# Two transformer blocks in float32 on one core: the out-projection of the first block's mixers taken over from float32 matmuls by three rounded passes

## What is computed

```python
h = rms_norm(x, mix_norm_g[l])
proj = jnp.einsum("bsd,dc->bsc", h, w_in[l])
moba_p, mla_p, sb_p, ssm_p = _split(proj, (MOBA_COLS, MLA_COLS, SB_COLS, SSM_COLS))
o_moba = moba_mixer(...); o_mla = mla_mixer(...)
o_sb = stick_breaking_mixer(sb_p); o_ssm = mamba2_mixer(...)
heads = rms_norm(jnp.stack([o_moba, o_mla, o_sb], axis=2), head_out_g[l])
mixed = jnp.concatenate([heads.reshape(bsz, seq, 3 * GROUP_WIDTH), o_ssm], axis=-1)
x = x + jnp.einsum("bsc,cd->bsd", mixed, w_out[l])
...                                   # then the feed-forward part of the layer
```

## Time and profile before

| | |
|---|---|
| three runs, median (lowest to highest) | 1769.16 us (1768.7 to 1773.98) |
| the profiled execution, its own time | 1764.72 us |
| span in the trace, first to last instruction | 1762.9 us |
| mean granted TensorE clock | 0.999 |
| TensorE matmul busy | 1747.6 us, 99% of the span |
| VectorE busy | 1191.3 us, 68% |
| ScalarE busy | 830.6 us, 47% |
| float32 matmuls of the out-projection (L892) | 256 records in two layers |

### The profile page before, as it was taken

The page is one execution under the profiler, slowest core; times in us unless marked ns, Lnnn a source line. Parts: engine busy times, 40 slices in busy tenths (PEclk is TensorE's granted clock), DMA queues, the critical chain, the costliest instruction groups (busy, mean ns, idle before and its releaser), DMA issues.

```text
span 1762.9 us, 32830 instructions
## 1 busy us (share of the span) xinstructions
PE 1747.6 (99%) x13378; PEld 1670.4 (95%) x13378; DVE 1191.3 (68%) x1863; ACT 830.6 (47%) x1108; POOL 29.2 (2%) x16
## 2 busy tenths in 40 slices
PE   8999999999999999999999999999999999999999
PEld 7879999988899999999989888999999999899999
DVE  6867886467698856766468623767556765777763
ACT  5656554356565544343345443343443344554442
POOL 0000000000000000000051000000000000000000
PEclk9999999999999999999999999999999999999999
DMA  6132556433145554455333422445444453335553
GB/s 257 73 144 106 195 183 224 168 112 143 72 168 190 209 205 167 169 190 186 127 134 144 168 84 96 169 183 208 166 156 178 167 203 144 109 138 194 188 211 122
DMA packets 36491, 284.28 MB, mean 161 GB/s; under 512 B 5040, under 2 KB 7344, under 8 KB 9008
## 3 DMA queue, kind: packets, MB, share of 16 engines
q1 hardware_dynamic: 36400, 283.00, 44.2%
HBM read 281.93 MB, written 1.05 MB: 161 GB/s over the span
## 4 chain that ended last, share of the span: by engine, by line
PE 88%; DVE 8%; ACT 2%; issue 1%; DMA 0%; SPq 0%; ACTq 0%; DVEq 0%
PE PS L1423 24%; PE PS L1428 24%; PE PS L1424 24%; PE PS L892 3%; PE PS L1301 3%; PE PS L727 1%; PE PS L771 1%; PE PS L748 1%; PE PS L1190 1%; PE PS L1089 0%; PE PS L916 0%; PE PS L1365 0%; DVE W L2577 0%; PE PS L1367 0%; PE PS L1371 0%
## 5 line engine op out<-in xcount | busy, mean ns | idle before, releaser
L1423 PE MATMUL PS<-Hhi,split 128*128 128x272 f32 (+1 forms) x2216 | 548.4, 286 | 0.0
L1424 PE MATMUL PS<-Hlo,split 128*128 128x272 f32 (+1 forms) x2120 | 520.1, 284 | 0.0
L2192 DVE TENSOR_TENSOR split<-wa,split 128x2048 fp32r<-128x2048 f32 (+2 forms) x174 | 358.7, 2061 | 123.9 <-ACT split L1567 123.9
L1423 PEld LDWEIGHTS PS<-Hhi,split 128*128 128x128 f32 x2216 | 416.4, 188 | 1.0 <-issue 0.4
L1424 PEld LDWEIGHTS PS<-Hlo,split 128*128 128x128 f32 x2120 | 399.1, 188 | 0.3
L1567 ACT CAST split<-wa 128x2048 fp32r<-128x2048 f32 (+2 forms) x174 | 299.3, 1720 | 63.9 <-PE PS L1428 61.4
L1428 PE MATMUL PS<-Hhi,split 128*128 128x256 f32 (+1 forms) x2080 | 274.8, 285 | 0.0
L1423 PE MATMUL PS<-hidhi,split 128*128 128x256 f32 (+1 forms) x1088 | 268.1, 285 | 0.5 <-DVE hidlo L2873 0.5
L1424 PE MATMUL PS<-hidlo,split 128*128 128x256 f32 (+1 forms) x1088 | 267.4, 284 | 0.0
L1428 PEld LDWEIGHTS PS<-Hhi,split 128*128 128x128 f32 x2080 | 261.9, 188 | 0.0
L1423 PEld LDWEIGHTS PS<-hidhi,split 128*128 128x128 f32 x1088 | 205.0, 188 | 1.0 <-DVE hidlo L2873 0.9
(11 more groups left out here) (422 smaller groups left out, 2380.5 us busy)
## 6 DMA issues: line engine op xcount, KB each, us to landing
wa<-in_wfi SPq DMA_DIRECT2D x126, 1024.0 KB, 4.8
wa<-in_wfo SPq DMA_DIRECT2D x48, 1408.0 KB, 6.1
wa<-in_wmix SPq DMA_DIRECT2D x25, 2048.0 KB, 7.9
wa<-in_wmix SPq DMA_DIRECT2D x4, 1536.0 KB, 6.4
H<-in_wfi SPq DMA_DIRECT2D x3, 1024.0 KB, 10.2
G<-in_wfi SPq DMA_DIRECT2D x3, 1024.0 KB, 5.0
wa<-in_wmix SPq DMA_DIRECT2D x2, 1024.0 KB, 4.7
wa<-in_wmix SPq DMA_DIRECT2D x1, 1824.0 KB, 7.6
```

What stands on the lines that cost most here:

```text
L1423: pe.matmul(o, hi, xhi, start=first, stop=False)
L1424: pe.matmul(o, hi, xlo, start=False, stop=False)
L2192: dve.tensor_tensor(out=wlo[n % 2][:, at:width], in0=wa[:, c % 2, at:width], in1=whi[n % 2][:, at:width].bitcast(F32), op=ALU.subtract).th ...
```

## The change

The out-projection goes over to rounded parts. Its weights become eight further pieces (numbers 16 to 23), one for each side and branch in the order of `OUT1`; ScalarE rounds each (`round_piece`) and VectorE forms its rest (`rest_piece`), placed by hand in the two streams. Two new places, M (over `Hlo`) and K (further on in `hidhi`), join A and B. Each branch's normed output is rounded by ScalarE (`round_branch`) and its rest formed by VectorE (`rest_of_branch`). On TensorE `rounded_rows` does hi*hi and lo*hi (16 matmuls) and `remaining_rows` hi*lo (8 matmuls), in place of the 8 float32 matmuls of `out_rows`. No DMA is added or removed, and the conditions on which slots are refilled stay (the out-projection's last matmuls of a side). First the tables and TensorE's stream:

```diff
+OUT1 = [(0, 2), (0, 1), (1, 2), (1, 1), (0, 3), (1, 3), (0, 0), (1, 0)]
+
 PIECES1 = [(1, 2), (1, 3), (2, 0), (2, 1), (2, 2), (2, 3), (3, 0), (3, 1), (3, 2), (3, 3), (4, 0), (4, 1), (4, 2), (4, 3), (5, 0), (5, 1)]
 
-PLACES1 = "AE" + "BCGH" + "AEBC" + "AEBG" + "EB"
+OUT_AT = len(PIECES1)
+PIECES1 = PIECES1 + [(6 + side, group) for side, group in OUT1]
+
+PLACES1 = "AE" + "BCGH" + "AEBC" + "AEBG" + "EB" + "AMBKAMBK"
+
+OUT_SPLITS = 1 + len(OUT1) // 2
...
+                def split_at(group):
+
+                    groups = [g for side, g in OUT1 if side == 0]
+                    return l * OUT_SPLITS + 2 + groups.index(group)
+
+                def rounded_rows(side, group, first=False):
+
+                    n = OUT_AT + OUT1.index((side, group))
+                    hi, lo = halves(n, 2)
+                    pe.wait_ge(S.mx_xhi, split_at(group))
+                    pe.wait_ge(S.mx_hi, pieces + n + 1)
                     for j in range(4):
-                        m = 4 * side + j
-                        for k in ks:
-                            mm = pe.matmul(out_place(m), wo[side][:, k, P * j:P * j + P], MIX[:, k, 0:SEQ],
-                                           start=first and m % 2 == 0 and k == ks[0], stop=last and k == ks[-1],
-                                           skip_group_check=True)
-                        if last and m % 2:
+                        for i in range(2):
+                            pe.matmul(out_place(4 * side + j), hi[:, i, P * j:P * j + P], Xhi[:, 2 * group + i, :],
+                                      start=first and j % 2 == 0 and i == 0, stop=False, skip_group_check=True)
+                    pe.wait_ge(S.mx_lo, pieces + n + 1)
+                    for j in range(4):
+                        for i in range(2):
+                            pe.matmul(out_place(4 * side + j), lo[:, i, P * j:P * j + P], Xhi[:, 2 * group + i, :],
+                                      start=False, stop=False, skip_group_check=True)
+
+                def remaining_rows(side, group, last=False):
+
+                    n = OUT_AT + OUT1.index((side, group))
+                    hi, _lo = halves(n, 2)
+                    pe.wait_ge(S.mx_xlo, split_at(group))
+                    for j in range(4):
+                        for i in range(2):
+                            mm = pe.matmul(out_place(4 * side + j), hi[:, i, P * j:P * j + P], Xlo[:, 2 * group + i, :],
+                                           start=False, stop=last and i == 1, skip_group_check=True)
+                        if last and j % 2:
                             mm.then_inc(S.prod_done, 1)
-
-                moba_rows, mla_rows, stick_rows, ssm_rows = ((2 * g, 2 * g + 1) for g in range(4))
+                    if not last:
+                        mm.then_inc(S.mx_used, 1)
...
                 soft_scores(moba, 0)
-                wo = [use(6, base, KD, P * PER1)]
-                pe.wait_ge(S.st_done, upto(S.st_done))
-                out_rows(0, stick_rows, first=True)
-                pe.wait_ge(S.ml_done, upto(S.ml_done))
+                take(2)
+                upto(S.st_done)
+                rounded_rows(0, 2, first=True)
+                upto(S.ml_done)
                 for h in range(4):
...
-                out_rows(0, mla_rows)
+                rounded_rows(0, 1)
+                remaining_rows(0, 2)
+                remaining_rows(0, 1)
                 soft_scores(moba, 1)
-                wo.append(use(7, base, KD, P * PER1))
                 pe.wait_ge(S.ssm_arg, upto(S.ssm_arg))
-                out_rows(1, stick_rows, first=True)
+                rounded_rows(1, 2, first=True)
+                remaining_rows(1, 2)
...
-                out_rows(1, mla_rows)
+                rounded_rows(1, 1)
+                remaining_rows(1, 1)
...
-                out_rows(0, ssm_rows)
+                rounded_rows(0, 3)
                 mean_square(head_norm(l, 0))
-                out_rows(1, ssm_rows)
+                rounded_rows(1, 3)
+                remaining_rows(0, 3)
+                remaining_rows(1, 3)
                 pe.wait_ge(S.mb_done, upto(S.mb_done))
-                out_rows(0, moba_rows, last=True)
-                out_rows(1, moba_rows, last=True)
+                for side in range(2):
+                    rounded_rows(side, 0)
+                    remaining_rows(side, 0, last=True)
...
+
+                def round_branch(group):
+
+                    ks = slice(2 * group, 2 * group + 2)
+                    act.copy(Xhi[:, ks, :], MIX[:, ks, 0:SEQ]).then_inc(S.mx_xhi, 1)
```

ScalarE's stream:

```diff
                 roots_of(qk_moba)
+                round_piece(16)
...
                 roots_of(head_norm(l, 1))
+                round_piece(17)
+                act.wait_ge(S.st_done, upto(S.st_done))
+                round_branch(2)
+                act.wait_ge(S.ml_done, upto(S.ml_done, 4))
+                round_branch(1)
                 soft_exp(moba, 0)
                 soft_copies(moba, 0)
+                round_piece(18)
                 act.wait_ge(S.ssm_arg, upto(S.ssm_arg))
                 act.activation(e0, x_ssm, ACT.Exp)
                 act.activation(e1[:, :, 0:P], e1[:, :, 0:P], ACT.Exp).then_inc(S.ssm_e, 1)
+                round_piece(19)
                 soft_exp(moba, 1)
+                round_piece(20)
                 act.wait_ge(S.ssm_y, upto(S.ssm_y))
                 squares_of(ssm_out(l))
+                round_piece(21)
                 soft_copies(moba, 1)
                 roots_of(ssm_out(l))
                 act.wait_ge(S.mb_pv, upto(S.mb_pv))
                 squares_of(head_norm(l, 0))
+                round_piece(22)
                 act.wait_ge(S.ss_done, upto(S.ss_done))
+                round_branch(3)
                 round_early(0)
                 roots_of(head_norm(l, 0))
+                round_piece(23)
+                act.wait_ge(S.mb_done, upto(S.mb_done, 2))
+                round_branch(0)
                 round_early(1)
```

VectorE's stream:

```diff
+                def rest_of_branch(group):
+
+                    ks, groups = slice(2 * group, 2 * group + 2), [g for side, g in OUT1 if side == 0]
+                    dve.wait_ge(S.mx_xhi, l * OUT_SPLITS + 2 + groups.index(group))
+                    dve.tensor_tensor(out=Xlo[:, ks, :], in0=MIX[:, ks, 0:SEQ], in1=Xhi[:, ks, :].bitcast(F32),
+                                      op=ALU.subtract).then_inc(S.mx_xlo, 1)
...
+                rest_piece(16)
                 turned_sum(qk_moba)
                 normalised(head_norm(l, 2)).then_inc(S.st_done, 1)
                 normalised(head_norm(l, 1)).then_inc(S.ml_done, 1)
+                rest_piece(17)
                 soft_max(moba, 0)
+                rest_of_branch(2)
+                rest_of_branch(1)
                 soft_divide(moba, 0)
+                rest_piece(18)
...
                 ins.then_inc(S.ssm_arg, 1)
+                rest_piece(19)
...
                 soft_max(moba, 1)
+                rest_piece(20)
...
                 dve.tensor_tensor(out=y, in0=y, in1=ZS[:, :, 0:SEQ], op=ALU.mult).then_inc(S.ssm_y, 1)
+                rest_piece(21)
                 soft_divide(moba, 1)
                 normalised(ssm_out(l)).then_inc(S.ss_done, 1)
+                rest_piece(22)
+                rest_of_branch(3)
...
+                rest_piece(23)
+                rest_of_branch(0)
                 rest_early(1)
```

19 lines of the change are left out of this document (10 added, 9 removed).

## The result

The changed kernel takes 1799.8 us (median of 4 runs, 1797.2 to 1802.1) beside 1768.9 us of the kernel before: ratio 1.0188, 95% interval 1.017 to 1.0206. That ratio is 33 us of change, two more than the 30.9 between these two medians, each of which is of four executions. The profiled execution took 1798.9 us with a span of 1797.1, 34.2 more than before.

The account below looks back on a forecast made before the run. TensorE, busy 99% of the span, was taken to bound the kernel. Waits of 13.4 us a layer, 27 in two, plus 4 for the clock made 31 us on 1769: 1800 us, range 1787 to 1810.

Parts of the forecast that it names:

- TensorE's saving: Out-projection: rounded matmuls take 24.0 us a layer for float32's 28.4, saving 4.4 if no engine is late.
- (g): From the ssm rows on: TensorE's 14.78 us of work becomes 12.6, giving 2.2 back.
- (a): Rests 16 and 17 on VectorE: scores 1.14 us late, tile 0's transposes 1.6 late; first rounded group at 109.6.
- (b): Cast and rest of piece 18 stand before the ssm arguments, which start at 118.48, 4.9 us late.
- (c): Cast and rest of piece 19 stand before the second ssm step: 7.0 us late; ssm values start at 127.6.
- (d): Cast and rest of piece 20, behind tile 1's exponentials, stand before VectorE's y: 10.65 us late.
- (e): Cast and rest of piece 21 stand before tile 1's division, 13.4 us late; its transposes come 13.1 late.
- (f): ScalarE's squares and casts before the rounded ssm branch: ssm rows at 146.81, another 2.5 us late.
- The clock: TensorE at half speed behind the 8.2 us gap before tile 1's transposes: +2 us a layer, 4 in all.
- it falls oftener: Rival: gaps before the ssm values and ssm rows also slow what follows, 4.9 us a layer; 1806 us, chance 0.09.
- The clock holds: Rival: TensorE keeps full clock through the gap, leaving the waits alone, +27 us; 1796 us, chance 0.24.
- Faster: Rival: pieces fill only ScalarE's and VectorE's idle time, TensorE keeps 4.4 us a layer; 1760 us, chance 0.04.

Follow-up runs that it names:

- run 1: The changed kernel with VectorE's rests 18 to 21 moved behind the steps each delayed, all work kept; 1779.7 us, ratio 1.0063.
- run 2: The changed kernel with only VectorE's rests 20 and 21 moved behind the division of tile 1; 1787.2 us, ratio 1.0122.
- run 3: The changed kernel with 32 idle matmuls a layer added ahead of TensorE's waits; 1790.6 us, ratio 1.0131.
- run 4: The changed kernel with the same casts, rests and groups on the same engines in another order; 1767.2 us, ratio 1.0002.
- run 5: Two versions of run 4's kernel: seven idle matmuls a layer added, 1762.6 us; first group left float32 ahead of the selection, 1762.0 us.
- run 6: Subtractions on GpSimd: all eight a layer, in nearly run 4's order, 1786.9 us; three of eight, in run 4's order, 1765.0 us.

## Why the prediction was right, point by point

The mechanism was right, and so were the sizes of the waits. The clock was priced near, but for falls in other places than those that came, and that the median of 1799.8 meets the forecast of 1800 is partly luck. Times of layer 0 of after are compared less 1.85 us, by which it started later, those of layer 1 less 17.47.

- **TensorE's saving and (g).** From the ssm rows to the norm sums 12.3 us (151.20 to 163.52) for a predicted 12.6. The rest of the 4.4 us was never to be seen, since TensorE waited in all the other stretches.
- **(a)** Scores 1.14 late, as predicted; first rounded group at 109.61 for 109.6. In layer 0 the transposes of tile 0 came 2.7 late for a predicted 1.6: the selection in front of them ran at half clock, which the prediction did not have. In layer 1 it ran at full clock, and they came 1.6 late.
- **(b), (c), (d)** Arguments at 120.0 for 118.5, second ssm step 126.4 for 124.9, values 129.2 for 127.6, y 135.9 for 134.4: all 1.5 late, the error of (a) handed on, each link of the predicted length. VectorE waited 3.08 us on the cast of `own_hi`, as foretold. Runs 1 and 2 show the links by undoing them.
- **(e)** Division at 140.5 for 139.0, gap 8.0 us for 8.2. In layer 1 the transposes of tile 1 came 13.3 late for a predicted 13.1.
- **(f)** TensorE idle 2.68 us before the ssm rows, where 0.22 were there before: the predicted 2.5. The rows start at 149.35 for 146.8, because transposes and mean square before them ran at half clock.
- **Sum of waits** 13.4 a layer; run 3, at full clock behind the gaps, has 13.5 twice.
- **The clock** was given 2 us a layer, all of it for the long gap. It took at least 2.2 and 3.6. In layer 0 only 1.1 come from the long gap (7.6 us from the transposes to the ssm rows for a predicted 6.5); 1.5 come from the fall at 113 us, which the prediction had no term for: it looked at gaps, and not at what kind of matmuls the change leaves between them. In layer 1 the gaps before the ssm values and the ssm rows brought half clock too, as in the rival "it falls oftener", which priced that at 4.9. So the term of 2 was near in layer 0 by errors that offset each other, and 1.6 short in layer 1.
- **The sum** was 31 us; the medians differ by 30.9. But the layers hold 32.8, the ratio says 33, and the kernel before measured 1766 in all later sets: the change was 2 us larger than forecast, and the four runs of before happened to read high.
- **Rivals.** "The clock holds" would have been 1796; run 3, where the idle matmuls held it up in the long gap, is 24.4 us above the kernel before (27.0 in the two layers) for that rival's 27. "Faster" failed as said: it needed (b) to (d) to vanish, and with nearly all of them gone (run 4) the time is only that of before, since the four steps that remain (two at the start, the division, the clock) eat 4.4 us a layer.

## What to carry to other kernels

When three engines hand a chain around and one is busy 99% of the time, added work on the others is priced by its place: the same 24 casts and 24 subtractions in two layers cost 33 us in one order and nothing in another. Put a piece behind the link that its engine owes next, and ask of each cast which subtraction waits for it. A cheaper form of filler work brings nothing where the chain, not the busy engine, sets the next start; take it only in the stretch behind the chain's last link (half of the change gave -1.8 us a layer, seven of its eight groups -1.1). And work that seems only to fill waits may hold up the clock.

## What the runs showed of the hardware that was not expected

- The granted clock fell to half while TensorE was busy without a break (run 5), in a stretch of 64-row, 4-row and few full matmuls, and stayed up over gaps of 0.3 to 1.65 us when a dense float32 group stood in that stretch. There idle time was neither needed nor enough. The Trainium skill ("TensorE: Matmul & The Clock Gate", Part 1) ties the full rate to sustained activity and the half rate to idleness. The half clock behind the gap of 8.04 us agrees; the fall of run 5, with no idle time, goes beyond what the page says. Which property of the dense group counts (its rows, or the time it takes) was not tried.
- One and the same gap does not always end alike: behind 2.68 us of idle time before the ssm rows the changed kernel ran at full clock in layer 0 (1.18 us for eight matmuls) and at half in layer 1 (1.95). What decides it is open.
- The clock also falls in some executions in a part that no kernel here changes. Windows of the kernel before, and of the order rearranged, whose execution was 4.2 us longer behind the two layers:

```profile
940.00:960.00 20.00, 19.11 (x174) 18.08 (x173) 14.97 (x34) 12.14 (x44) 0.00 (x0) 1.00 0.35 116
```

```profile
940.00:960.00 20.00, 17.63 (x140) 16.38 (x140) 13.21 (x35) 8.06 (x27) 0.00 (x0) 0.83 0.29 106
```

  Three traces have it: runs 1, 3 and 4 have a mean clock of 0.98 from 900 to 1100 us where the others have 1.00, and the stretch behind their two layers is 3 to 4 us longer. That is about half of the spread of one kernel (1763 to 1771). Why the versions of run 5 had fewer long executions than that of run 4 stays open.
- VectorE operations with two SBUF operands wait out whole GpSimd instructions (0.47 us becomes 2.57), and those that read PSUM don't: 1.22 us for a row of 1024 columns with a subtraction on GpSimd beside it, in run 6 with three rests there:

```profile
105.44 1.22 DVE L2379 TENSOR_TENSOR more<-PS,rope 128x1024 f32<-128x1024 f32 x1
```

```profile
104.51 2.37 POOL L2194 TENSOR_TENSOR wa_lo<-wa,own_hi 128x1024 fp32r<-128x1024 f32 x1 [104.06 <-ACT own_hi L1721]
```
